# Projection units contraction-outermost, modulation weights in buffers of their own, unread matmuls at the start

## The chip, the cores and the metric

The kernel runs on one core of a Trainium2 chip. The metric is the device time of one execution in microseconds (us). The engines are TensorE (PE; its weight loads are PEld), VectorE (DVE), ScalarE (ACT), GpSimd (POOL) and SyncE (SP), which here only issues DMAs. PSUM has 8 banks of 128 x 512 floats.

## The reference, cut to what matters

One layer of a decoder on 256 prompt tokens and 32 sample tokens (8 sequences of 4), 288 token columns in all, width 1024, everything in float32:

```
mod = silu(c) @ w_ada + b_ada             # 9 rows of c (1 prompt, 8 samples); 6 x 1024 columns
sh1, sc1, g1, sh2, sc2, g2 = mod
h = x * (1 + sc1) + sh1
qa, ka, va, qb, kb, vb, ga, gb = split(h @ w_in)      # 1024 x 5120
... rotary on q and k; dilated window attention (3 groups) and block attention ...
merged = sigmoid(ga) * (oa @ w_pa) + sigmoid(gb) * (ob @ w_pb)
x = LayerNorm(alpha * x + g1 * (merged @ w_o))
f = silu(gt) * up,  up, gt = split((x * (1 + sc2) + sh2) @ w_up)
y = LayerNorm(alpha * x + g2 * (f @ w_down))
```

The first 3072 columns of w_in are q, k and v of the attention: 24 blocks of 128 columns. Blocks 0 to 5 are q of branch A, 6 to 11 k, 12 to 17 v, 18 and 19 q of branch B, 20 and 21 k, 22 and 23 v. The keys, values and window buffers are outputs too.

## The kernel before, in words

Activations lie transposed: width on the partitions (KT = 8 row blocks k), the 288 tokens as columns. A product is made of half units. A half unit gives 128 output columns: for each of the 8 row blocks three matmuls (`mm3`: high part by high part, high by low, low by high), 24 matmuls of 128x128 by 288 into one PSUM bank (`unit_mm`). The weights' high part is a copy that rounds (`w_hi`, ScalarE, `split_hi`), the low part the rest (`w_lo`, VectorE, `split_lo`). Both have 4 places (`SPLIT`) and are made 4 half units ahead (`AHEAD`). The rounded h is `act_hi`, its rest `act_lo`.

Weights come in tiles of 1 MiB: 1024 rows by 256 columns, which are two half units. They go through a ring `raw` of 3 places (`RAW`), in one order of tiles n. SP issues all of them in that order; before each it waits until the place is free (`free_slot`): the tile three before has been split, or, for a tile of adaLN weights, multiplied. The adaLN weights are 24 tiles of the same ring. Tiles 0 to 7 are the adaLN chunks of sh1 and sc1. After them, a w_in tile and an adaLN tile take turns until the 12 w_in tiles of q, k and v are through, with masks, tables and the keys of sequences 0 to 3 in between. The last four adaLN tiles are taken later (`ADA1`, `ADA2`).

An adaLN chunk is multiplied by `ada_mm`: silu(c) as the stationary operand, 32 columns wide, in four column groups of the array, each holding two row blocks. ScalarE copies the bank (`ada_rows`), TensorE adds the four groups and turns the result (`ada_turn`), VectorE adds the bias (`ada_add`) into `mod`.

TensorE's order is written out by hand. At first it turns c, the rows of b_ada and ln1, multiplies chunks 0 to 7 (in the order `ADA_FIRST`), with x turned after the fourth (`turn_x`). VectorE then modulates: h[k] from x, sc1 and sh1, two row blocks a time (`modulate_pair`); ScalarE rounds h (`h_leading`), VectorE makes the rest (`rest_of`). The first half unit needs all 8 row blocks of h, and so all 8 chunks. Then come 12 pairs of half units c, hh into banks 0 and 1, an adaLN chunk and its turn in each pair. A bank is evicted by ScalarE (with rotary work of VectorE and GpSimd behind it for the blocks of q and k), or by VectorE for v. After the last pair TensorE transposes v and k, then the keys of the sample caches, and the attention follows. Later stages wait on counts of these semaphores.

The lines of the profile: L664 to L666 are the three matmuls of `mm3`; L689 `ada_mm`; L697 `ada_turn`; L710 and L713 the turns of c and rows; L718 and L723 `turn_x`; L768 the transposes of v and k; L473 and L478 the splits; L533 the issue of a tile; L1121 `ada_rows`; L1375 `ada_add`; L1387 the modulation; L1392 `rest_of`.

Of the kernel before, what the change touches and what calls it, by code (L numbers as in the profile page):

```python
# [36 lines left out]
SPLIT = 4  # L37
N_ADA0 = 8
MIX0 = N_ADA0
GATE0 = MIX0 + 24  # L40
# [119 lines left out]
ADA_FIRST = (0, 4, 1, 5, 2, 6, 3, 7)  # L160


def ada_chunk(n):

    if n < MIX0:
        return ADA_FIRST[n]
    if n < GATE0:
        return N_ADA0 + (n - MIX0) // 2 if (n - MIX0) % 2 else None
# [17 lines left out]
MIX_N = 12  # L186
# [91 lines left out]
def build(nc, x_prompt, x_sample, cache_a, cache_rows, cache_b, page_table, c_prompt, c_sample, w_ada, b_ada, w_in,  # L278
# [24 lines left out]
    kvin, _ = sb("kvin", [128, 2, 6, 256])  # L303
# [7 lines left out]
    rowbuf, _ = sb("rowbuf", [128, 3, 256])  # L311
# [3 lines left out]
    rows, _ = sb("rows", [64, 128])  # L315
# [42 lines left out]
    st6, _ = sb("st6", [128, 3, 4, 6])  # L358
# [19 lines left out]
    c_zero, c_ready, ada_used, first_in = sem("c_zero"), sem("c_ready"), sem("ada_used"), sem("first_in")  # L378
# [81 lines left out]
    def part(t, slot, by_rows):  # L460
        if by_rows:
            return t[:, slot, :]
        return t[:, slot, :].rearrange("p (k n) -> p k n", k=8)

    def split_hi(act, nb, slot4, rslot, hh, need, by_rows=False):

        if isinstance(nb, int) and nb == 0:
            act.wait_ge(first_in, 16)
        else:
            act.wait_ge(raw_in[rslot], need)  # L470
# [10 lines left out]
    def halves(first, last):  # L481

        out = []
        for n in range(first, last):
            by_rows = PAB0 <= n < WO0 or n >= DOWN0
# [17 lines left out]

    PAB_BANK = (0, 1, 6, 3)
# [14 lines left out]
    def _(sp):  # L519
# [14 lines left out]

        def load_ada(n):
            a = ada_chunk(n)
            load(n, n % RAW, w_ada_v[:, :, 256 * a:256 * a + 256], raw8(n % RAW))

        for n in range(MIX0):
            load_ada(n)  # L540
            if n == 0:
                sp.dma_start(rows[0:48, :], b_ada.rearrange("a (j p) -> (a j) p", p=128)).then_inc(rows_in, 16)
                sp.dma_start(rows[48:56, :], ln1_g.rearrange("a (j p) -> (a j) p", p=128)).then_inc(rows_in, 16)
                sp.dma_start(rows[56:64, :], ln1_b.rearrange("a (j p) -> (a j) p", p=128)).then_inc(rows_in, 16)
            if n == 2:
                sp.dma_start(x_tok[:, 0:2, :], x_prompt.rearrange("a (t p) d -> p (a t) d", p=128)).then_inc(x_in, 16)
                sp.dma_start(x_tok[0:SAMPLE, 2, :], x_sample.rearrange("b t d -> (b t) d")).then_inc(x_in, 16)
# [39 lines left out]
        for n in range(MIX0, GATE0):  # L587
            c = (n - MIX0) // 2
            if n == MIX0:
                free_slot(n)  # L590
                sp.dma_start(raw8(n % RAW)[:, :, 0:128], w_in_v[:, :, 0:128]).then_inc(first_in, 16)
                sp.dma_start(raw8(n % RAW)[:, :, 128:256], w_in_v[:, :, 128:256]).then_inc(raw_in[n % RAW], 16)
                sp.dma_start(cst[:, C_COS:C_MS], const[:, C_COS:C_MS]).then_inc(tables_in, 16)
                sp.dma_start(pages[:], page_table.rearrange("b n -> (b n)").unsqueeze(0)).then_inc(pages_in, 16)
            elif ada_chunk(n) is None:
                load(n, n % RAW, w_in_v[:, :, 256 * c:256 * c + 256], raw8(n % RAW))
            else:
                load_ada(n)
            if n == MIX0 + 9:
                sp.dma_start(cst[:, C_MS:C_END], const[:, C_MS:C_END]).then_inc(masks_in, 16)  # L600
                sp.wait_ge(pages_in, 16)
            if MIX0 + 9 <= n < MIX0 + 9 + DEC_B:
                look_up_pages(n - MIX0 - 9)
            if n > MIX0 + 9 and n % 2 and (n - MIX0 - 11) // 2 < 4:
                load_kv((n - MIX0 - 11) // 2, 0)
# [72 lines left out]
    def ada_bank(i):  # L678
        return {20: 5, 21: 4, 22: 7, 23: 2}.get(i, 5 + i % 3)

    def ada_mm(pe, n):

        i, slot, bank = N_ADA_BEFORE[n], n % RAW, ada_bank(N_ADA_BEFORE[n])
        pe.wait_ge(raw_in[slot], raw_need(n, slot))
        if i >= 3:
            pe.wait_ge(ada_mod, i - 2)
        for k in range(KT):
            q = 32 * (k % 4)
            mm = nc.tensor.matmul(psum[q:q + 32, bank, 0:256], c_z[:, k, :], raw8(slot)[:, k, :], start=(k < 4), stop=(k >= 4),  # L689
                                  skip_group_check=True)  # L690
# [15 lines left out]
    def _(pe):  # L706
        pe.wait_ge(const_in, 16)
# [3 lines left out]
        mm.then_inc(turned_c, 1)  # L711
        pe.wait_ge(rows_in, 48)
# [16 lines left out]
        for i in range(N_ADA0):  # L729
            ada_mm(pe, i)  # L730
            if i >= 1:
                ada_turn(pe, i - 1)
            if i == 3:
                pe.wait_ge(rows_ready, 1)
                turn_x()
        ada_turn(pe, N_ADA0 - 1)

        for c in range(MIX_N):
            for hh in range(2):
                u = 2 * c + hh  # L740
                if c >= 1 and hh == 0 or u == 1:
                    ada_mm(pe, MIX0 + 2 * c + 1)
                if c >= 1:
                    pe.wait_ge(acc_free[hh], c)
                unit_mm(pe, u, u % SPLIT, hh, h_lo if u == 0 else None)
            if c < MIX_N - 1:
                ada_turn(pe, N_ADA0 + c)

        for j in range(8):
            g, hp = j // 2, j % 2  # L750
            if j == 2:
                ada_turn(pe, N_ADA0 + MIX_N - 1)
# [17 lines left out]
        pe.wait_ge(ada_mod, N_ADA0 + MIX_N)  # L770
# [172 lines left out]
        ada_mm(pe, ADA1)  # L943
        pe.wait_ge(o_ready, N_UNITS)
        outputs_turn(1)
        ada_mm(pe, ADA1 + 1)
        ada_turn(pe, 20)


        for h in range(4):  # L950
# [18 lines left out]
            if h == 0:  # L969
                ada_turn(pe, 21)  # L970
# [55 lines left out]
        ada_mm(pe, ADA2)  # L1026
        ada_mm(pe, ADA2 + 1)
        ada_turn(pe, 22)
        ada_turn(pe, 23)


        def first_up_pair():
# [3 lines left out]
            for k in range(KT):  # L1036
                pe.wait_ge(h2_lo, H2_LO_AT[k])
                for q in range(3):
                    wh, wl = part(w_hi, q, False), part(w_lo, q, False)
# [3 lines left out]
            unit_mm(pe, H_UP + 3, 3, UP_BANK[3])  # L1043

        def up_pair(j, second=False):
            for q in range(4):
# [7 lines left out]
                unit_mm(pe, nb, q, q % 2)  # L1054
# [35 lines left out]
        for hcol in range(2):  # L1090
            for kk in range(0, FT if hcol == 0 else FT - 6, 2):
# [5 lines left out]
                if hcol == 1 and kk == 0:  # L1097
                    pe.wait_ge(ada_mod, 24)
# [15 lines left out]
    def _(act):  # L1114
# [12 lines left out]
        for i in range(N_ADA0):  # L1127
            ada_rows(i)
            if i == 4:
                for j in range(2):  # L1130
                    act.wait_ge(turned_x, j + 1)
                    nc.scalar.activation(xT[:, 4 * j:4 * j + 4, 0:128], psum[:, 1 + j, :].rearrange("p (k c) -> p k c", c=128),
                                         ACT.Copy).then_inc(x_ready_act, 1)
            if i == 6:
                for k in range(6):
                    h_leading(k)
        hi_static(act, H_MIX)
        h_leading(6)
        h_leading(7)
        for nb in range(H_MIX + 1, H_MIX + AHEAD):  # L1140
            hi_static(act, nb)

        for c in range(MIX_N):
            for hh in range(2):
                nb = H_MIX + 2 * c + hh
                if c >= 1 and hh == 0:
                    ada_rows(N_ADA0 + c)
# [5 lines left out]
                if nb == H_MIX:  # L1153
                    ada_rows(N_ADA0)
# [54 lines left out]
        for s in range(1, 16):  # L1209
# [77 lines left out]
        ada_rows(22)  # L1287
        ada_rows(23)
# [632 lines left out]
```

## Time and profile before

| | |
|---|---|
| time, median of 3 runs | 564.42 us (560.51 to 568.14) |
| the profiled execution's own time | 561.89 us |
| its span | 560.3 us |
| TensorE matmuls busy | 516.1 us, 92% |
| VectorE, ScalarE, GpSimd busy | 290.5, 223.5, 92.2 us |
| DMA | 116.78 MB, mean 208 GB/s |

The span is what the profiler shows of one execution; all stages below lie on its clock. Busy time of TensorE is the time in which some matmul is under way. Matmuls overlap, so what one costs in a stream is read from the distance of two starts, not from the duration that a row shows. The granted clock is the share of full speed that the record gives for a stretch.

### The profile page before, as it was taken

To read this page: it belongs to the slowest core of one execution; us is meant where nothing else is said; L and a number is where in the kernel's file an instruction comes from. 1 tells how busy PE (TensorE), PEld (TensorE's weight loads), DVE (VectorE), ACT (ScalarE), POOL (GpSimd) and SP (SyncE) were. 2 spreads that over 40 slices of the span, in tenths; PEclk is the share of its full clock that TensorE was granted. 3 is DMA by queue.
4 is the path that set the end of the run, shared out by engine and by line. 5 is a ranking of instruction groups with operands and counts; after the bars stand their busy time and mean duration, and the time that the engine had idled before them with its cause. 6 is when DMAs were issued, how large, how long until landed. Compare 5 with 4: busy or idle time off the path is not lost.

```text
span 560.3 us, 10315 instructions
## 1 busy us (share of the span) xinstructions
PE 516.1 (92%) x4051; PEld 473.0 (84%) x4051; DVE 290.5 (52%) x561; ACT 223.5 (40%) x377; POOL 92.2 (16%) x127
## 2 busy tenths in 40 slices
PE   4787999999999989999989979999999999999990
PEld 2546899989978979897789869999999999999980
DVE  0055657556743453353587595546555544435356
ACT  1042424333344454253643645465444344333311
POOL 1000123002770000000055053601111100000005
PEclk9999899999999999998999979999999999999995
DMA  8987699998185982194433474898876745354002
GB/s 280 340 267 231 208 359 348 338 303 293 38 285 173 303 279 77 42 274 142 151 116 114 148 225 132 302 329 289 264 278 216 272 159 182 120 187 171 17 1 84
DMA packets 96719, 116.78 MB, mean 208 GB/s; under 512 B 3596, under 2 KB 87756, under 8 KB 96165
## 3 DMA queue, kind: packets, MB, share of 16 engines
q1 hardware_dynamic: 94788, 102.76, 56.3%
q0 software_dynamic: 1888, 13.44, 6.6%
q8 instruction: 30, 0.49, 0.4%
q14 instruction: 13, 0.10, 0.1%
HBM read 112.90 MB, written 13.57 MB: 226 GB/s over the span
## 4 chain that ended last, share of the span: by engine, by line
PE 77%; DMA 9%; DVE 4%; ACT 3%; SPq 2%; issue 2%; POOL 2%; POOLq 0%; DVEq 0%; ACTq 0%
PE psum L664 21%; PE psum L666 20%; PE psum L665 20%; DMA raw<-in_w_in 6%; PE psum L689 3%; PE psum L784 3%; DMA raw<-in_w_ada 2%; PE psum L900 2%; PE psum L697 2%; PE psum L844 1%; PE psum L886 1%; DVE w_lo L478 1%; PE psum L853 1%; PE psum L798 1%; ACT qkvg L1206 1%
## 5 line engine op out<-in xcount | busy, mean ns | idle before, releaser
L478 DVE TENSOR_TENSOR w_lo<-raw,w_hi 128x1024 fp32r<-128x1024 f32 x118 | 146.7, 1244 | 169.6 <-ACT w_hi L473 169.4
L664 PE MATMUL psum<-act_hi,w_hi 128*128 128x288 f32 x736 | 223.9, 304 | 9.2 <-DVE act_lo L1647 3.5
L665 PE MATMUL psum<-act_lo,w_hi 128*128 128x288 f32 x736 | 219.6, 298 | 0.0
L666 PE MATMUL psum<-act_hi,w_lo 128*128 128x288 f32 x736 | 219.0, 298 | 0.0
L473 ACT ACTIVATE w_hi<-raw 128x1024 fp32r<-128x1024 f32 x118 | 124.1, 1056 | 138.3 <-PE psum L666 90.7
L664 PEld LDWEIGHTS psum<-act_hi,w_hi 128*128 128x128 f32 x736 | 140.5, 191 | 17.9 <-issue 11.0
L666 PEld LDWEIGHTS psum<-act_hi,w_lo 128*128 128x128 f32 x736 | 141.0, 192 | 0.0
L665 PEld LDWEIGHTS psum<-act_lo,w_hi 128*128 128x128 f32 x736 | 140.8, 191 | 0.1
L664 PE MATMUL psum<-f_hi,w_hi 128*128 128x288 f32 x176 | 52.4, 298 | 0.6 <-DVE f_t L1685 0.6
L665 PE MATMUL psum<-f_lo,w_hi 128*128 128x288 f32 x176 | 51.9, 295 | 0.0
L666 PE MATMUL psum<-f_hi,w_lo 128*128 128x288 f32 x176 | 51.8, 294 | 0.0
L1789 POOL TENSOR_TENSOR qkvg<-qkvg,cst 128x288 f32 (+1 forms) x16 | 16.6, 1036 | 121.0 <-ACT qkvg L1150 121.0
L689 PE MATMUL psum<-raw,c_z 128*32 128x256 f32 x384 | 32.4, 468 | 4.4 <-DMA raw<-in_w_ada 4.3
L664 PEld LDWEIGHTS psum<-f_hi,w_hi 128*128 128x128 f32 x176 | 33.0, 187 | 0.9 <-issue 0.8
L666 PEld LDWEIGHTS psum<-f_hi,w_lo 128*128 128x128 f32 x176 | 33.1, 188 | 0.0
L665 PEld LDWEIGHTS psum<-f_lo,w_hi 128*128 128x128 f32 x176 | 33.0, 188 | 0.0
L1823 POOL TENSOR_TENSOR qkvg<-qkvg,gated 128x288 f32<-128x288 f32 x8 | 8.4, 1079 | 120.0 <-DVE gated L1597 120.0
L697 PEld LDWEIGHTS psum<-cst,rowbuf 128*128 128x128 f32 x96 | 16.0, 235 | 11.9 <-ACT rowbuf L1121 6.2
L1874 POOL DMA_DIRECT2D out<-in_cache_kv_a x24 | 11.7, 488 | 77.4 <-PE psum L666 75.8
L689 PEld LDWEIGHTS psum<-raw,c_z 128*32 128x32 f32 x384 | 11.5, 125 | 13.3 <-DMA raw<-in_w_ada 5.4
L1314 ACT ACTIVATE silu_t<-psum 128x288 f32<-128x288 f32 x22 | 9.0, 409 | 33.5 <-PE psum L666 33.5
L697 PE MATMUL psum<-cst,rowbuf 128*128 128x9 f32 x96 | 16.7, 284 | 5.0 <-ACT rowbuf L1121 5.0
(190 smaller groups left out, 556.4 us busy)
## 6 DMA issues: line engine op xcount, KB each, us to landing
raw<-in_w_ada SPq DMA_DIRECT2D x24, 1024.0 KB, 7.1
raw<-in_w_up SPq DMA_DIRECT2D x22, 1024.0 KB, 7.0
raw<-in_w_in SPq DMA_DIRECT2D x19, 1024.0 KB, 7.0
raw<-in_w_down SPq DMA_DIRECT2D x10, 1024.0 KB, 5.0
out<-in_cache_kv_a POOLq DMA_DIRECT2D x16, 504.0 KB, 6.1
raw<-in_w_o SPq DMA_DIRECT2D x4, 1024.0 KB, 4.8
kvin<-in_cache_kv_a SPq DMA_DIRECT2D x8, 256.0 KB, 3.1
kvin<-in_cache_kv_b SPq DMA_DIRECT2D x16, 128.0 KB, 3.4
```

Of the source, the lines that this page charges most:

```text
L473: nc.scalar.activation(part(w_hi, slot4, by_rows), raw_half(rslot, hh, by_rows), ACT.Copy).then_inc(hi_ready, 1)
L478: nc.vector.tensor_tensor(part(w_lo, slot4, by_rows), raw_half(rslot, hh, by_rows), part(w_hi, slot4, by_rows).bitcast(F32), ALU.subtract) ...
L664: nc.tensor.matmul(out, hi_l, hi_r, start=start, stop=False, skip_group_check=True)
L665: nc.tensor.matmul(out, hi_l, lo_r, start=False, stop=False, skip_group_check=True)
L666: return nc.tensor.matmul(out, lo_l, hi_r, start=False, stop=stop, skip_group_check=True)
L689: mm = nc.tensor.matmul(psum[q:q + 32, bank, 0:256], c_z[:, k, :], raw8(slot)[:, k, :], start=(k < 4), stop=(k >= 4), skip_group_check=True)
L697: mm = nc.tensor.matmul(psum[:, ada_bank(i), 256 + 9 * hh:256 + 9 * hh + 9], rowbuf[:, i % 3, 128 * hh:128 * hh + 128], cst[:, C_ADA:C_ADA ...
L784: mm = nc.tensor.transpose(psum[:, bank, col:col + nr], kv_tiles(b, 0, tile)[0:nr, 0, 128 * hp:128 * hp + 128], cst[0:nr, 0:nr])
L900: mm = nc.tensor.matmul(psum[:, 6, E * i:E * i + E], prbT[:, u % 2, 128 * n:128 * n + 128], tok[:, kb, 1, 256 * g + E * h:256 * g + E * h ...
L1314: nc.scalar.activation(silu_t[:, q, :], psum[:, q, 0:TOK], ACT.Silu).then_inc(silu_ready, 1)
L1789: nc.gpsimd.tensor_tensor(block_at(qkvg, blk), block_at(qkvg, blk), cst[:, C_COS:C_COS + TOK], ALU.mult).then_inc(cos_done, 1)
L1874: pool.dma_start(kv_sample[g][bass.ds(b, 1), 0:BUF[g] - DEC_T, :], cache_rows[g][bass.ds(b, 1), DEC_T:BUF[g], :]).then_inc(moved, 16)
```

## The change

- **Order of the projections.** Blocks 12 to 17 (v of branch A) are made first and together (`first_mm`): for each row block k, the 18 matmuls of six output blocks into six banks (0 to 5). Their weights come in four tiles of two row blocks by 768 columns (`load_first`), split one row block a time. Row block k needs only h[k]. After that come the other nine pairs (`MIX_C`), as before into banks 0 and 1.
- **adaLN weights.** They come as 24 parts of 512 rows by 512 columns, of which the first 20 have five buffers of their own (`ada_s`, laid over memory that is free then, by `ADA_BUF`), and no longer pass through the ring. SP waits for the buffer's last use. Two parts make a chunk of 512 columns: 12 chunks, evictions and `ada_add`s for 24, each with twice as many columns. Chunks 0 and 2 (shift and scale of row blocks 0 to 3) are first.
- **Unread matmuls.** `keep_warm` multiplies the identity with 256 columns into bank 5; nobody reads it. 12 of them stand between the first pieces of work.
- **Order of loads.** The loads of SP up to the first gate tile are written out by hand. The keys of sequences 0 to 3 are loaded after the last adaLN part.
- The four last adaLN tiles stay in the ring, as parts; semaphore counts and places follow.

```diff
+MIX_C = (0, 1, 2, 3, 4, 5, 9, 10, 11)
+FIRST_BLK, FIRST_N = 12, 6
+FIRST_COLS = 128 * FIRST_N
-ADA_FIRST = (0, 4, 1, 5, 2, 6, 3, 7)
+ADA_ORDER = (0, 2, 1, 3, 4, 5, 6, 7, 8, 9, 10, 11)
+ADA_BANK = (6, 7, 6, 7, 6, 7, 6, 7, 6, 7, 5, 7)
+ADA_BUF = (0, 1, 2, 3, 4, 0, 1, 2, 3, 4, 2, 3, 4, 2, 3, 4, 2, 4, 2, 4)
+MIX_ADA = [range(N_ADA0 + (4 * m + 2) // 3, N_ADA0 + (4 * m + 6) // 3) for m in range(9)]
...
+    ada_s = [sb(f"ada_s{i}", [128, 4, 512], F32, o)[0]
+             for i, o in enumerate((o_qkvg + 8 * TOK * 4, o_qkvg + 8 * TOK * 4 + 8192, o_qkvg + 24 * TOK * 4, o_kvin, o_tmp + 4096))]
...
+        def load_start(q):
+            last = [p for p in range(q) if ADA_BUF[p] == ADA_BUF[q]]
+            if last:
+                sp.wait_ge(ada_used, last[-1] + 1)
+            sp.dma_start(ada_s[ADA_BUF[q]][:], ada_part(q)).then_inc(start_in[ADA_BUF[q]], 16)
+
+        def load_first(n):
+            dst = raw[:, n % RAW, 0:2 * FIRST_COLS].rearrange("p (k n) -> p k n", k=2)
+            load(n, n % RAW, w_in_v[:, 2 * n:2 * n + 2, 128 * FIRST_BLK:128 * FIRST_BLK + FIRST_COLS], dst)
+
+        load_start(0)
...
+        load_start(1)
+        sp.dma_start(x_tok[:, 0:2, :], x_prompt.rearrange("a (t p) d -> p (a t) d", p=128)).then_inc(x_in, 16)
+        sp.dma_start(x_tok[0:SAMPLE, 2, :], x_sample.rearrange("b t d -> (b t) d")).then_inc(x_in, 16)
+        load_start(2)
+        load_start(3)
+        load_start(4)
+        load_start(5)
+        load_first(0)
+        load_first(1)
+        load_start(6)
+        load_start(7)
+        load_first(2)
+        load_first(3)
...
+        load_start(8)
+        load_start(9)
+        load_mix(0)
+        load_start(10)
+        load_mix(1)
+        load_mix(2)
+        load_mix(3)
+        load_start(11)
...
+        load_mix(7)
+        load_start(17)
+        load_start(18)
+        load_mix(8)
+        load_start(19)
+        load_kv(0, 0)
+        load_kv(1, 0)
+        sp.wait_ge(ada_used, 19)
+        load_kv(2, 0)
+        sp.wait_ge(ada_used, 20)
+        load_kv(3, 0)
...
+    def ada_mm(pe, q, src, arrived, need):
+        i, a = q // 2, q % 2
+        pe.wait_ge(arrived, need)
+        if a == 0 and i >= 2:
+            pe.wait_ge(ada_mod, i - 1)
+        for kk in range(4):
+            mm = nc.tensor.matmul(psum[32 * kk:32 * kk + 32, ADA_BANK[i], :], c_z[:, 4 * a + kk, :], src[:, kk, :],
+                                  start=(a == 0), stop=(a == 1), skip_group_check=True)
+        mm.then_inc(ada_used, 1)
...
+    def first_mm(pe, k):
+        pe.wait_ge(lo_ready, k + 1)
+        pe.wait_ge(h_lo, k + 1)
+        for q in range(FIRST_N):
+            c = 128 * q
+            mm = mm3(psum[:, q, 0:TOK], w_hi[:, k % SPLIT, c:c + 128], w_lo[:, k % SPLIT, c:c + 128], act_hi[:, k, :], act_lo[:, k, :],
+                     k == 0, k == KT - 1)
...
+        def keep_warm(n):
+            for _ in range(n):
+                nc.tensor.matmul(psum[:, 5, 0:256], ident, cst[:, 0:256], start=True, stop=True, skip_group_check=True)
...
+        keep_warm(4)
...
+        ada_start(pe, 0)
+        keep_warm(2)
+        ada_start(pe, 1)
+        keep_warm(1)
+        ada_turn(pe, 0)
+        keep_warm(2)
+        pe.wait_ge(rows_ready, 1)
+        turn_x()
+        ada_start(pe, 2)
+        keep_warm(2)
+        ada_start(pe, 3)
+        keep_warm(1)
+        ada_turn(pe, 1)
+        ada_start(pe, 4)
+        ada_start(pe, 5)
+        first_mm(pe, 0)
+        ada_turn(pe, 2)
+        first_mm(pe, 1)
+        ada_start(pe, 6)
+        ada_start(pe, 7)
+        first_mm(pe, 2)
+        ada_turn(pe, 3)
+        for k in range(3, KT):
+            first_mm(pe, k)
+
+        for m in range(9):
+            for q in MIX_ADA[m]:
+                ada_start(pe, q)
+            for hh in range(2):
+                nb = H_MIX + 2 * m + hh
+                pe.wait_ge(acc_free[hh], m + 1)
+                unit_mm(pe, nb, nb % SPLIT, hh)
+                if hh == 0 and m in ROWS_AT:
+                    ada_turn(pe, ROWS_AT[m])
```

In ScalarE's and VectorE's order, `hi_static(k)` and `lo_static(k)` of the eight row blocks stand between `h_leading` and `rest_of` of the same row blocks; `modulate_pair(0)` and `(1)` wait for two chunks of `mod`, `(2)` and `(3)` for four. The splits of the first three half units of the pairs stand ahead of the evictions of the six banks, which ScalarE and VectorE share.

## Rows read from the trace of the kernel before

**Rows 1.** The page, busy time of TensorE, us (share) xinstructions.

```profile
PE 516.1 (92%) x4051; PEld 473.0 (84%) x4051; DVE 290.5 (52%) x561; ACT 223.5 (40%) x377; POOL 92.2 (16%) x127
```

**Rows 2.** Windows: stretch, its length, busy us, granted clock, DMA share, GB/s.

```profile
0.00:25.00 25.00, 13.63 (x94) 8.11 (x95) 1.27 (x7) 3.06 (x6) 2.71 (x7) 1.00 0.96 308
25.00:44.00 19.00, 15.06 (x101) 9.31 (x99) 10.26 (x32) 7.12 (x16) 0.00 (x0) 1.00 0.93 286
44.00:54.00 10.00, 9.97 (x64) 9.12 (x64) 5.43 (x8) 2.69 (x4) 0.79 (x1) 1.00 0.57 179
54.00:66.00 12.00, 8.71 (x63) 7.97 (x62) 5.49 (x11) 4.33 (x7) 1.90 (x2) 0.86 0.87 282
66.00:147.00 81.00, 80.30 (x688) 74.01 (x687) 49.39 (x106) 26.98 (x42) 17.44 (x36) 1.00 0.87 289
80.00:115.00 35.00, 35.00 (x301) 32.56 (x299) 20.95 (x43) 11.09 (x18) 7.05 (x6) 1.00 1.05 347
512.00:514.00 2.00, 2.00 (x17) 2.00 (x16) 1.93 (x5) 0.41 (x1) 0.00 (x0) 1.00 0.97 375
```

**Rows 3.** TensorE in order of time, 0 to 45: start, us, instruction, idle before.

```profile
3.85 0.99 PE L710 MATMUL psum<-cst,ctok 9*128 9x9 f32 x8 [3.85 <-DMA ctok<-in_c_sample]
...
23.12 3.65 PE L718 MATMUL psum<-cst,x_tok 128*128 128x128 f32 x16
...
36.15 1.94 PE L689 MATMUL psum<-raw,c_z 128*32 128x256 f32 x16
...
44.03 0.61 PE L664 MATMUL psum<-act_hi,w_hi 128*128 128x288 f32 x1 [3.17 <-DVE w_lo L478]
44.44 0.44 PE L665 MATMUL psum<-act_lo,w_hi 128*128 128x288 f32 x1
44.68 0.44 PE L666 MATMUL psum<-act_hi,w_lo 128*128 128x288 f32 x1
```

**Rows 4.** The same of 57 to 148.

```profile
57.43 0.61 PE L697 MATMUL psum<-cst,rowbuf 128*128 128x9 f32 x4 [3.29 <-ACT rowbuf L1121]
...
58.97 0.40 PE L664 MATMUL psum<-act_hi,w_hi 128*128 128x288 f32 x1
...
66.99 0.51 PE L697 MATMUL psum<-cst,rowbuf 128*128 128x9 f32 x4
67.43 1.07 PE L689 MATMUL psum<-raw,c_z 128*32 128x256 f32 x16
68.43 0.40 PE L664 MATMUL psum<-act_hi,w_hi 128*128 128x288 f32 x1
...
71.72 0.30 PE L664 MATMUL psum<-act_hi,w_hi 128*128 128x288 f32 x1
...
147.09 0.30 PE L666 MATMUL psum<-act_hi,w_lo 128*128 128x288 f32 x1
```

**Rows 5.** Waits of 0 to 160 (total, times, longest); the chain of waits near 108.

```profile
ACT w_hi L473 <- DMA raw<-in_w_in: 39.3, 11, 6.7
...
108.56 8.82 DMA raw<-in_w_in
```

**Rows 6.** VectorE in order of time, 38 to 44.

```profile
38.30 0.74 DVE L1387 TENSOR_SCALAR qkvg<-xT,mod 128x256 f32<-128x256 f32 x2
...
42.76 1.22 DVE L478 TENSOR_TENSOR w_lo<-raw,w_hi 128x1024 fp32r<-128x1024 f32 x1
43.89 0.82 DVE L1392 TENSOR_TENSOR act_lo<-qkvg,act_hi 128x288 fp32r<-128x288 f32 x2
```

**Rows 7.** TensorE in order of time, first pair of the up projection.

```profile
328.02 0.58 PE L664 MATMUL psum<-act_hi,w_hi 128*128 128x288 f32 x1 [3.50 <-DVE act_lo L1647]
...
332.79 0.29 PE L666 MATMUL psum<-act_hi,w_lo 128*128 128x288 f32 x1
332.92 0.29 PE L664 MATMUL psum<-act_hi,w_hi 128*128 128x288 f32 x1
```

**Rows 8.** DMA issues of the page: count, KB each, median us to landing.

```profile
raw<-in_w_in SPq DMA_DIRECT2D x19, 1024.0 KB, 7.0
```

More of the change, by code:

```diff
@@ L465, in split_hi @@
     def split_hi(act, nb, slot4, rslot, hh, need, by_rows=False):
[L467 to L470, printed above, removed]
+        act.wait_ge(raw_in[rslot], need)
         if not isinstance(nb, int) or nb >= SPLIT:
@@ L484, in halves @@
         for n in range(first, last):
-            by_rows = PAB0 <= n < WO0 or n >= DOWN0
+            by_rows = "first" if n < MIX0 else PAB0 <= n < WO0 or n >= DOWN0
             for hh in range(n_halves(n)):
@@ L533, in load, with ada_part @@
             sp.dma_start(dst, src).then_inc(raw_in[slot], 16)
+        def ada_part(q):
+            j, a = ADA_ORDER[q // 2], q % 2
+            return w_ada_v[:, 4 * a:4 * a + 4, 512 * j:512 * j + 512]
         def load_ada(n):
[L536 to L547, printed above, removed]
+            load(n, n % RAW, ada_part(ada_chunk(n)), raw4(n % RAW))
@@ L585, in load_static, with load_mix @@
                 load(n, n % RAW, w_up_v[:, :, col:col + 256], raw8(n % RAW))
[L587 to L605, printed above, removed]
+        def load_mix(m):
+            n, c = MIX0 + m, MIX_C[m]
+            load(n, n % RAW, w_in_v[:, :, 256 * c:256 * c + 256], raw8(n % RAW))
+        load_start(8)
[6 more added lines that the diff above has]
+        load_start(11)
+        sp.dma_start(cst[:, C_MS:C_END], const[:, C_MS:C_END]).then_inc(masks_in, 16)
+        sp.wait_ge(pages_in, 16)
+        look_up_pages(0)
+        look_up_pages(1)
+        load_mix(4)
+        load_start(12)
+        look_up_pages(2)
+        look_up_pages(3)
+        load_mix(5)
+        load_start(13)
+        load_start(14)
+        look_up_pages(4)
+        look_up_pages(5)
+        load_mix(6)
+        load_start(15)
+        load_start(16)
+        look_up_pages(6)
+        look_up_pages(7)
+        load_mix(7)
[9 more added lines that the diff above has]
+        load_kv(3, 0)
         load_static(GATE0)
@@ L1038, in first_up_pair @@
                 for q in range(3):
-                    wh, wl = part(w_hi, q, False), part(w_lo, q, False)
+                    wh, wl = (part(w, (H_UP + q) % SPLIT, False) for w in (w_hi, w_lo))
                     mm = mm3(psum[:, UP_BANK[q], 0:TOK], wh[:, k, :], wl[:, k, :], act_hi[:, k, :], act_lo[:, k, :], k == 0, k == KT - 1)
@@ L1420, in _ @@
+        lo_static(dve, 5)
         rest_of(qkvg, 6, h_hi, h_lo)
         rest_of(qkvg, 7, h_hi, h_lo)
-        for nb in range(H_MIX + 1, H_MIX + AHEAD):
+        for nb in range(6, 11):
             lo_static(dve, nb)
+        for q in (1, 3, 5):
+            if q < 5:
+                dve.wait_ge(first_done, q + 1)
+            else:
+                dve.wait_ge(half_used, KT)
+            V.tensor_copy(qkvg[:, FIRST_BLK + q, :], psum[:, q, 0:TOK]).then_inc(acc_free[1] if q == 1 else v_free, 1)
```

266 lines of the change are left out of this document (135 added, 131 removed).

## The prediction, made before the result was known

> **What bounds the kernel now.** I read the page's busy table first: TensorE works 516 of 560 us [rows 1]. So time can only come from its idle time, from its slow stretches, or from fewer matmuls. The change leaves the real matmuls as they are (118 half units' worth, the same adaLN columns, the same row turns), so I looked for idle and slow stretches with a table of windows by stage [rows 2]. From 66 to 147 us TensorE is busy 80.3 of 81 us. There is nothing to win there but an earlier start. In the first 44 us it is busy 28.7, and with preparations only; from 54 to 66 it is busy 8.7 of 12.
>
> The list of TensorE's instructions in order of time shows what it does [rows 3]. The first projection matmul starts at 44.03, after a wait of 3.17 us for the split weights. Until then it turns and multiplies adaLN chunks as they land, and waits. Neighbouring matmuls of 288 columns are 0.24 us apart there, which is the 1.2 GHz level (288 / 0.24 us), though the granted column says 1.00. Later they are 0.13 us apart, the 2.4 GHz level [rows 7]. The same list from 57 us on gives the prices at the full level [rows 4]: a half unit 3.29 us (68.43 to 71.72), an adaLN chunk 1.00 (67.43 to 68.43), a pair of turns 0.44 (66.99 to 67.43). The stage ends at about 147.2 (last start 147.09). At full price it is 24 x 3.29 + 12 x 1.00 + 11 x 0.44 = 95.8 us; it takes 103.2. The 7.4 lost are the first half unit at the lower level (24 x 0.24 = 5.8 for 3.29), the wait of 3.29 that ends at 57.43 and the slow unit behind it, and a wait near 117. The list of waits has their origin: ScalarE's split waits 39 us in sum for w_in, and one such load took 8.82 us [rows 5].
>
> So the stage ends at (start of projections) + (TensorE's work) + (waits), and the start is set by DMA. 0 to 25 us brings 7.7 MB, and the stream then runs at 347 GB/s where the engines are saturated [rows 2]. All 8 MiB of the adaLN weights of shift and scale, x, and a weight tile must be in first.
>
> **The change, part by part.** All times below are on the clock of the profiled run (span 560.3, time 561.9; the median of the three runs is 564.4, so 2.5 more).
>
> *Start.* The contraction-outermost block k needs only its own h[k] and 768 columns of row block k. h[0..3] need adaLN chunks 0 and 2 (4 MiB), but two more MiB are issued before w_in. The first tile is thus complete after 6.3 MB of adaLN, 1.2 of x, 0.2 of small loads (7.7 MB: 25 us as before) and 0.8 MB more: 25 + 0.79/0.347 = 27.3 us. The new adaLN loads have runs of 2 KB, as w_down's, which reach 375 GB/s in a slice at share 0.97, against 347 at 1.05 for runs of 1 KB [rows 2]. With 375 it is 25.6. I take 26. Split at three quarters of 1.22 us [rows 6] and of the 1.05 that the high part takes, the first projection matmul is at 28.
>
> *Does TensorE get there in time?* The twelve unread matmuls (256 columns, fp32, whole array) have no row. Lower bound: two transposes of 128 columns, 3.65/16 x 2 = 0.46 us at the lower level. Upper: an adaLN part does eight such matmuls in four column groups in 1.94; if the four run at once, one alone is 0.24 x 4 = 0.97 [rows 3]. I take 0.9 at the lower level, 0.45 at the full one, since these are fp32 matmuls and not transposes. Chain at the lower level: c turned at 4.8, four unread 3.6, rows 0.4, chunk part 0 1.9, two unread 1.8, part 1 1.9: 14.4. From there at the full level: unread 6 x 0.45, turns 2 x 0.88, x 2.4, parts 2 x 1.0 = 8.9: 23.3, and modulation 0.2 + 1.2 = 24.7. That is before 28, so the unread matmuls cost nothing; their cover is the arrival of w_in tile 0. At the lower level throughout it is 14.4 + 17.8 + 1.4 + 1.3 (split and rest) = 35: the cover is gone.
>
> *The block of six.* 8 x 18 matmuls. Block 0 at 0.24 us: 28 to 32.3. Turns 1.4: 33.7. Block 1 at full 2.4: 36.1. Adding parts 6 and 7 (landed at 26 + 2.9/0.35 = 34.3) 2.0: 38.1. Block 2: 40.5, turns 41.4, block 3: 43.8. Block 4 waits for the third and fourth chunks: add 0.2, two modulations 2.4 (one is 0.74 [rows 6] and two small steps of the samples, about 0.23 each), split 0.9, rest 0.4: 45.3, a new stall of 1.5 us. Blocks 4 to 7: 54.9. Before, this work (six half units) was done at about 75.
>
> *The nine pairs.* 18 x 3.29 + 12 x 1.00 + 6 x 0.88 = 76.5 us. Evicting six banks at once adds no wait of TensorE: bank 0 is done 2 us before the block ends, and two adaLN parts (2.0 us) come first. DMA has to bring 7.3 MB of w_in, 9.4 of adaLN, 1.3 of masks, 2.9 of keys and 2.1 of gates: 23 MB, 66 us at 347 GB/s, under 76.5. SP's queue is in order, and its tightest place is part 17: it may be issued only when part 15 is used (start of pair 5) and is wanted at the start of pair 6, 8.5 us later; a w_in load's median from issue to landing is 7.0 [rows 8]. Part 18 and the last w_in tile stand behind it. I put 1 us for such waits, between 0 and 7.4, what the old stage lost. End: 54.9 + 76.5 + 1 = 132.4, against 147.2. Gain 14.8.
>
> *The rest.* The key loads 0 to 3 move behind the last adaLN part, 2.9 MB or 8.4 us; the first is wanted some 6 us after the stage's end (the 24 transposes of v and k). The fourth may be issued only when part 19 is used, at the start of the ninth pair (124), some 13 us before it is wanted. I cost this at nothing; the last pair and the transposes cover it, and without them it would be up to those 8.4 us. Later stages move as a block, since their waits count TensorE's progress. The later adaLN turns (20 to 23) become two and save at most 0.9; I take 0. The two doubled semaphore counts, the rowbuf's size and st6's new place: nothing, no engine waits on them.
>
> Sum: 561.9 - 14.8 = 547.1 in a run like the profiled one, 549.6 against the median. I say 548.
>
> **A rule against this change.** The first of the blocks walks six PSUM banks, three matmuls in each. The up projection's first pair walks three banks in the same way, and after 4.4 us at the lower level its matmuls are 0.13 us apart [rows 7], so the trace has no fall with cycling. The Trainium skill, "TensorE: Matmul & The Clock Gate", section "A second HAM failure mode: psum-queue depth-cycling", says that going through PSUM banks makes TensorE micro-idle between groups and swing between its two clock levels. By that rule the sum would be case C below.
>
> **Rivals.**
> A. *The unread matmuls do not raise the clock.* Before, TensorE is busy without a gap from 23 to 39 and a chunk still takes 1.94 at 36.15, not 1.00 [rows 3, 4]; the turns of rows and x are among the new work too. For the full level: the six parts are denser with the unread ones between. Then block 0 starts at 35, not 28: 554.
> B. *Loads arrive just late, or the gain is given back behind the stage.* Part 17 or the last w_in tile costs two waits like that at 54 to 57, or the keys come late: 7 us back, 554.
> C. *Bank cycling.* 144 x (0.24 - 0.133) = 15.4 us: 562, no change.
> D. *Slower.* ScalarE splits weights and evicts banks in one order. A late w_in load blocks its split, the eviction behind it waits, then TensorE, and after a wait of 3 us it runs at the lower level (the unit from 58.97 [rows 4] took 4.8, not 3.3). Price 3.6 + 1.5 = 5.1 us for each pair it hits. The place is SP's queue, where w_in loads now stand behind loads that wait for TensorE's use of an adaLN buffer. It decides from three pairs on (15.3 of 14.8); with five it is 547.1 + 25.5 = 573. Against it: 66 us of DMA in 76.5, and five buffers more.
>
> Chances: forecast 0.60, A 0.17, B 0.10, C 0.05, D 0.08. **Range**: below, no stall at all, 395 GB/s and the 0.9 of the turns: 543; above, A and B with the median's 2.5 and some noise: 560. C and D are left out. **Signs**: 2% of 564.4 is 11.3 us, about what a measurement here can tell, so faster means under 553.1. Forecast nearly all, a bit of B: faster 0.61. A, B, C and the lesser half of D: 0.34. Slower by over 2% needs D in six pairs or more: 0.05.
>
> **What would show it.** Steps right: first projection matmul near 28 with a short wait for w_lo before it; parts 2 to 5 in 1.0 us each, not 1.9 (else A); the ninth pair's end near 132, TensorE nearly gapless from 55 on; a spacing of 0.13 in blocks 1 to 7 (else C). Wrong: waits of TensorE for adaLN parts 16 to 19 or of ScalarE for w_in in the pairs (B, D); a first projection matmul at 35; or the stage ends at 132 while the stretch from there to the end, 413 us now, has grown.

## The result, and the profile after

The changed kernel takes 568.68 us in the median of 4 runs (566.3 to 569.54), the kernel before 563.97 (560.51 to 568.14): ratio 1.0099, 95% interval 1.0058 to 1.014. It is 1% slower; 548 was forecast. The profiled execution of the changed kernel took 566.3 us, span 564.7. All ratios, here and below, leave out an execution that took over 1.5% longer than the fastest of the same kernel; medians and ranges take in every one.

The windows of the changed kernel by stage (stretch, length, busy us of TensorE, its weight loads, VectorE, ScalarE, GpSimd, granted clock, DMA share, GB/s) answer to [rows 2]:

```profile
0.00:25.00 25.00, 18.94 (x113) 11.16 (x113) 3.94 (x13) 3.80 (x6) 2.70 (x7) 1.00 0.92 333
25.00:44.00 19.00, 15.58 (x109) 13.11 (x110) 8.02 (x20) 6.93 (x13) 0.00 (x0) 0.91 1.04 407
44.00:66.00 22.00, 20.43 (x157) 17.85 (x155) 14.31 (x24) 10.88 (x18) 0.80 (x1) 1.00 0.97 336
66.00:124.00 58.00, 58.00 (x440) 50.09 (x440) 39.47 (x84) 19.57 (x30) 12.38 (x14) 1.00 0.76 265
124.00:157.00 33.00, 19.52 (x116) 17.51 (x108) 15.43 (x31) 7.04 (x20) 11.36 (x26) 0.74 0.33 100
```

From 66 to 124 us TensorE works without a gap; then it is busy 19.5 of 33 us, at a clock granted at 0.74. Its instructions in order of time show both parts (they answer to [rows 3, 4]):

```profile
29.48 0.58 PE L721 MATMUL psum<-act_hi,w_hi 128*128 128x288 f32 x1 [3.23 <-DVE act_lo L1493]
...
34.63 0.29 PE L723 MATMUL psum<-act_hi,w_lo 128*128 128x288 f32 x1
34.76 0.29 PE L721 MATMUL psum<-act_hi,w_hi 128*128 128x288 f32 x1
...
136.39 1.88 PE L756 MATMUL psum<-cst,rowbuf 128*128 128x9 f32 x8 [8.39 <-ACT rowbuf L1213]
...
139.71 0.44 PE L721 MATMUL psum<-act_hi,w_hi 128*128 128x288 f32 x1
139.95 0.44 PE L722 MATMUL psum<-act_lo,w_hi 128*128 128x288 f32 x1
...
150.21 0.66 PE L862 MATMUL psum<-cst,qkvg 128*128 128x128 f32 x2 [5.09 <-DVE tok L1592]
...
156.54 1.96 PE L878 MATMUL psum<-cst,kvin 128*128 128x128 f32 x12
```

The first projection matmul starts at 29.48 instead of 44.03. The first half of the ninth pair, the last but one unit, ends near 127.9. One turn (0.9) and one half unit (3.3) are left, so the stage could end at 132.0. Instead TensorE waits 8.39 us for a copy of ScalarE, does most of the last half unit with starts 0.24 us apart (the 1.2 GHz level), ends at 143.2, and after fifteen transposes waits 5.09 us more for VectorE's tok copies, which take the transposed k out of PSUM. The key turns (the transposes of the sample caches' keys) begin at 156.5, where the kernel before began them at 153.0:

```profile
153.00 1.96 PE L784 MATMUL psum<-cst,kvin 128*128 128x128 f32 x12
```

What ScalarE did (L484 is the split, L1255 the eviction, L1213 `ada_rows`):

```profile
120.46 0.41 ACT L1255 ACTIVATE qkvg<-psum 128x288 f32<-128x288 f32 x1 [1.22 <-PE psum L723]
133.55 1.06 ACT L484 ACTIVATE w_hi<-raw 128x1024 fp32r<-128x1024 f32 x1 [12.68 <-DMA raw<-in_w_in]
134.51 0.39 ACT L1255 ACTIVATE qkvg<-psum 128x288 f32<-128x288 f32 x1
134.81 1.05 ACT L484 ACTIVATE w_hi<-raw 128x1024 fp32r<-128x1024 f32 x1
135.75 0.59 ACT L1213 ACTIVATE rowbuf<-psum 128x512 f32<-128x512 f32 x1
```

It waits 12.68 us for a w_in tile, to split it; the eviction of the eighth pair's second bank and the adaLN copy stand behind it in its order. The last half unit needs that bank too, and by the code it is free only when VectorE has read it behind the eviction (L1544, the rotary work), which stands behind the low part of the same split (L489):

```profile
134.64 1.23 DVE L489 TENSOR_TENSOR w_lo<-raw,w_hi 128x1024 fp32r<-128x1024 f32 x1 [10.11 <-ACT w_hi L484]
...
135.79 0.48 DVE L1544 STREAM_SHUFFLE rope_t<-psum 128x288 f32<-128x288 f32 x1
```

SP's queue shows which tile it is, and why it is late:

```profile
119.29 0.97 SPq L600 DMA_DIRECT2D k_early<-in_cache_kv_b  x2
124.68 0.34 SPq L594 DMA_DIRECT2D k_late<-in_cache_kv_a  x1
...
126.27 1.91 SPq L600 DMA_DIRECT2D k_late<-in_cache_kv_b  x2
128.22 1.06 SPq L545 DMA_DIRECT2D raw<-in_w_in  x2
```

It is the first gate tile. Between 120 and 124.7 SP waits for adaLN part 19 to be used, because the keys of sequence 3 go into memory that overlaps that part's buffer; the gate tile stands behind them and leaves at 128.22. The kernel before issued it at 132.93, but 14 us before its stage ended; here it is 4 us before the time at which the stage could have ended. The line of the kernel before:

```profile
132.93 2.09 SPq L533 DMA_DIRECT2D raw<-in_w_in  x2
```

VectorE and GpSimd near the second wait (L1559 are the copies of the last queries, L1921 the scaling of x):

```profile
143.86 5.56 DVE L1559 COPY qz<-qkvg 64x32 f32<-64x32 f32 x4
149.46 0.42 DVE L1591 COPY tok<-psum 128x256 f32<-128x256 f32 x1
```

```profile
142.78 6.04 POOL L1921 TENSOR_SCALAR xT<-xT 128x2304 f32<-128x2304 f32 x1
```

Four copies of 64x32 take 5.56 us. They end when GpSimd's 6 us instruction ends. The tok copies that TensorE waits for come after them. In the kernel before the same four took 0.81 us and were done before the scaling began:

```profile
143.29 0.81 DVE L1443 COPY qz<-qkvg 64x32 f32<-64x32 f32 x4
```

```profile
147.39 6.04 POOL L1809 TENSOR_SCALAR xT<-xT 128x2304 f32<-128x2304 f32 x1
```

### The profile page after: what moved, and what is told of

It reads as the page before. It is cut to its first block, busy times and chain, and to the rows that moved or that the text cites. A ratio compares the mean times of both kernels' runs of the same rounds, so it can differ in the third digit from the quotient of the medians.

```text
span 564.7 us, 9951 instructions
## 1 busy us (share of the span) xinstructions
PE 514.8 (91%) x3883; PEld 468.6 (83%) x3883; DVE 294.7 (52%) x548; ACT 223.1 (40%) x370; POOL 89.3 (16%) x127
## 4 chain that ended last, share of the span: by engine, by line
PE 79%; DMA 8%; DVE 5%; issue 2%; ACT 2%; SPq 2%; POOL 1%; POOLq 0%; ACTq 0%; DVEq 0%
PE psum L721 21%; PE psum L722 20%; PE psum L723 20%; DMA raw<-in_w_in 4%; DMA raw<-in_w_up 3%; PE psum L742 3%; PE psum L878 3%; PE psum L994 2%; PE psum L756 1%; PE psum L980 1%; ACT w_hi L484 1%; PE psum L938 1%; PE psum L947 1%; DVE qz L1559 1%; PE psum L892 1%
## 5 line engine op out<-in xcount | busy, mean ns | idle before, releaser
L489 DVE TENSOR_TENSOR w_lo<-raw,w_hi 128x1024 fp32r<-128x1024 f32 (+1 forms) x120 | 147.1, 1228 | 163.3 <-ACT w_hi L484 163.0
L484 ACT ACTIVATE w_hi<-raw 128x1024 fp32r<-128x1024 f32 (+1 forms) x120 | 124.6, 1041 | 129.1 <-PE psum L723 97.4
L1901 POOL TENSOR_TENSOR qkvg<-qkvg,cst 128x288 f32 (+1 forms) x16 | 14.7, 920 | 118.3 <-ACT qkvg L1255 118.3
L756 PEld LDWEIGHTS psum<-cst,rowbuf 128*128 128x128 f32 x96 | 12.6, 203 | 11.2 <-ACT rowbuf L1213 11.2
L742 PE MATMUL psum<-ada_s,c_z 128*32 128x512 f32 x160 | 20.5, 602 | 1.5 <-DMA ada_s<-in_w_ada 1.4
L756 PE MATMUL psum<-cst,rowbuf 128*128 128x9 f32 x96 | 12.7, 260 | 9.3 <-ACT rowbuf L1213 9.1
L1255 ACT ACTIVATE qkvg<-psum 128x288 f32<-128x288 f32 x16 | 6.5, 408 | 35.2 <-PE psum L723 35.2
```

Of the source, the lines that this page charges most:

```text
L489: nc.vector.tensor_tensor(part(w_lo, slot4, by_rows), raw_half(rslot, hh, by_rows), part(w_hi, slot4, by_rows).bitcast(F32), ALU.subtract) ...
L742: mm = nc.tensor.matmul(psum[32 * kk:32 * kk + 32, ADA_BANK[i], :], c_z[:, 4 * a + kk, :], src[:, kk, :], start=(a == 0), stop=(a == 1), s ...
L756: mm = nc.tensor.matmul(psum[:, ADA_BANK[i], 9 * hh:9 * hh + 9], rowbuf[:, i % 2, 128 * hh:128 * hh + 128], cst[:, C_ADA:C_ADA + 9], start ...
L1901: nc.gpsimd.tensor_tensor(block_at(qkvg, blk), block_at(qkvg, blk), cst[:, C_COS:C_COS + TOK], ALU.mult).then_inc(cos_done, 1)
```

## The experiments

Two causes were to be shown: **G**, the gate tile behind the keys' wait, and **Q**, the copies of the last queries under GpSimd's scaling. Each was taken out of the changed kernel alone (e1; e2 and e6), both together (e3), and each put into the kernel before alone (e8, e7). Ratios are to the kernel before, run on the same chip beside it.

**e1: the gate tile earlier.**

```diff
         load_start(19)
+        load_static(GATE0)
         load_kv(0, 0)
         load_kv(1, 0)
+        load_static(GATE0 + 1)
...
         load_kv(3, 0)
-        load_static(GATE0)
-        load_static(GATE0 + 1)
```

> The changed kernel with one edit in SP's order: the first gate tile is loaded right after adaLN part 19, the second after the keys of sequence 1, so that neither stands behind the wait for part 20. Theory G+Q (two new waits at the end of the pairs; G: the gate tile stands behind the keys' wait, its split blocks ScalarE's evictions; Q: VectorE's copies of the last queries are blocked by GpSimd's scaling of x): ScalarE's wait of 12.7 us for w_in goes, TensorE's wait of 8.4 us too, the ninth pair ends near 132 (now 143.1), but Q stays and still costs TensorE about 5 us and a slow stretch: 10 us less than the changed kernel, 556 to 559. Rival K (the gain cannot be had: the keys come later by as much, or DMA is short there): the key turns wait instead, 564 to 568.

Measured: 553.71 us (546.94 to 559.76), ratio 0.9872 (0.9805 to 0.9939). ScalarE and TensorE:

```profile
122.12 1.06 ACT L484 ACTIVATE w_hi<-raw 128x1024 fp32r<-128x1024 f32 x1 [1.46 <-DMA raw<-in_w_in]
```

```profile
131.71 0.38 PE L862 MATMUL psum<-cst,qkvg 128*128 128x128 f32 x2
...
139.71 0.66 PE L862 MATMUL psum<-cst,qkvg 128*128 128x128 f32 x2 [6.06 <-DVE tok L1592]
```

The wait of 8.4 us is gone, the stage ends at 131.7. The copies of the queries now take 6.54 us, and TensorE waits 6.1 for the tok copies. G is real, and Q stays, as expected. The time is a little below the range and scatters.

**e2: the copies of the last queries after the eighth pair.** The edit is `if m == 8:` to `if m == 7:` before `queries_by_row(3)`.

> The changed kernel with one edit in VectorE's order: the copies of the last queries stand after the eighth pair, not after the ninth. Theory G+Q: TensorE's wait of 5.1 us for the tok copies goes, and the transposes run at 0.11 us a matmul, not 0.21, so 6 to 8 us less than the changed kernel: 560 to 562; the wait of 8.4 us stays. Rival K: GpSimd's scaling blocks another copy of VectorE instead, under 2 us less.

Measured: 559.22 us (558.49 to 561.85), ratio 0.9984 (0.9953 to 1.0015), just below the 560 to 562 expected. VectorE and GpSimd in e2:

```profile
137.88 0.81 DVE L1559 COPY qz<-qkvg 64x32 f32<-64x32 f32 x4
...
143.27 0.43 DVE L1591 COPY tok<-psum 128x256 f32<-128x256 f32 x1
143.61 0.27 DVE L1592 COPY tok<-psum 32x128 f32<-32x128 f32 x1
```

```profile
142.00 6.04 POOL L1921 TENSOR_SCALAR xT<-xT 128x2304 f32<-128x2304 f32 x1
```

The copies take 0.81 us ahead of the scaling. The tok copies, which read PSUM, run at their usual 0.43 and 0.27 us in the middle of it. Of the copies seen here only those from SBUF to SBUF were held up. The wait of 8 us stays; the key turns begin 5.4 us after the stage's end (142.4 to 147.8), not 13.4.

**e3: both.**

> Both edits. Theory G+Q: no wait of TensorE over 1 us between 47 and 150, ninth pair ends near 132, the time is what was predicted for the change, 546 to 552. The two gains add up: 16 to 19 us less than the changed kernel. Rival K: 558 to 568.

Measured: 547.54 us (546.51 to 549.15), ratio 0.9779 (0.9713 to 0.9845). TensorE in e3, at the stage's end:

```profile
124.56 1.06 PE L742 MATMUL psum<-ada_s,c_z 128*32 128x512 f32 x8
128.85 0.96 PE L756 MATMUL psum<-cst,rowbuf 128*128 128x9 f32 x8
132.93 0.38 PE L862 MATMUL psum<-cst,qkvg 128*128 128x128 f32 x2
...
138.32 1.96 PE L878 MATMUL psum<-cst,kvin 128*128 128x128 f32 x12
```

The stage ends at 132.9 without a wait, the key turns begin 5.4 us later. The forecast for the change was 547.1 in such a run, with the stage's end at 132.4: it is the time of this kernel, which differs from the changed one in the places of two loads and of four small copies. That the two agree within 0.5 us is partly luck: the block of six ended 1.9 us later than forecast (56.8, not 54.9), and the nine pairs took 1.4 us less than the 77.5 put down for them and their waits.

**e4: both, without the unread matmuls.** All calls of `keep_warm` are left out.

> Both edits, and the twelve unread matmuls left out. Theory W0 (block 0 waits for DMA and the split anyway; the unread matmuls buy little): the first chunks run at the lower level, block 0 starts 1 to 2 us later than in e3, the time is 0 to 3 us more than e3's. Rival W1 (they carry the start): block 0 starts at 33 or later and the blocks stay slow longer, 5 us or more above e3. Rival W2 (they cost): faster than e3.

Measured: 545.50 us (543.12 to 547.8), ratio 0.974 (0.9667 to 0.9812): by the medians not slower than e3 but 2 us faster, though the two ranges overlap. W1 is out. TensorE in e4:

```profile
7.88 1.93 PE L742 MATMUL psum<-ada_s,c_z 128*32 128x512 f32 x8
11.33 1.94 PE L742 MATMUL psum<-ada_s,c_z 128*32 128x512 f32 x8 [1.51 <-DMA ada_s<-in_w_ada]
13.98 1.88 PE L756 MATMUL psum<-cst,rowbuf 128*128 128x9 f32 x8 [0.72 <-ACT rowbuf L1207]
...
19.91 1.92 PE L742 MATMUL psum<-ada_s,c_z 128*32 128x512 f32 x16
...
25.09 1.07 PE L742 MATMUL psum<-ada_s,c_z 128*32 128x512 f32 x8 [0.48 <-DMA ada_s<-in_w_ada]
```

Parts 0 and 1 run at the lower level (1.93 and 1.94 us), but parts 2 and 3, which take 1.92 us together, and part 5 (1.07) at the full one, with no unread matmul before them; and block 0 starts at 29.38, against 29.48 in the changed kernel. e10 and e11 repeat the pair.

**e5: the block of six waits for all of h.** On e3; in ScalarE's and VectorE's order h[4..7] go ahead of the fifth split.

```diff
-        first_mm(pe, 0)
         ada_turn(pe, 2)
-        first_mm(pe, 1)
         ada_start(pe, 6)
         ada_start(pe, 7)
-        first_mm(pe, 2)
         ada_turn(pe, 3)
-        for k in range(3, KT):
+        pe.wait_ge(h_lo, KT)
+        for k in range(KT):
             first_mm(pe, k)
```

> The kernel with both edits (e3), but the block of six waits for all eight row blocks of h, as the kernel before did: TensorE multiplies and turns chunks 1 and 3 first, ScalarE and VectorE round h[4..7] before the fifth split. Theory O (contraction-outermost order is worth its overlap): the first projection matmul moves from 29.5 to 38 to 40, blocks 1 to 7 run without a stall, the block of six ends at 60 to 62 (now 57), the time is 3 to 6 us above e3's 547.5. Rival N (the order is worth nothing, the early weights and separate buffers are all): within 1.5 us of e3.

Measured: 556.01 us (555.63 to 556.27), ratio 0.9892 (0.9861 to 0.9923), 8.5 us above e3. The first projection matmul moves to 42.6 and the block of six ends at 63.5 (e3: 56.8). Theory O holds, with more than the 3 to 6 us expected. Not all of it is the lost overlap: the third chunk's turn waits 5.64 us for ScalarE's copy, which stands behind the first splits in its order, and the turn behind that wait and part of the adaLN work after it are at the lower level. How much each of these costs was not taken apart.

**e6: the scaling waits for the copies of the queries.** On the changed kernel; one line in GpSimd's order, `pool.wait_ge(qz_ready, 4)`, ahead of the scaling of x.

> The changed kernel with one wait more on GpSimd: it scales x only after VectorE has copied all queries; nothing else is moved. Theory Q (the last queries' copies are blocked by GpSimd's 6 us instruction while it runs): the four copies take 0.8 us, not 5.6, TensorE's wait of 5.1 us for the tok copies goes: 560 to 562. Rival Q2 (the copies stand too late, whatever GpSimd does; the place in VectorE's order is the cause): the copies stay slow or the wait stays, 566 to 569.

Measured: 560.89 us (558.61 to 564.45), ratio 0.9986 (0.9959 to 1.0014). The copies stand where the change put them, and VectorE does them in:

```profile
144.69 0.73 DVE L1559 COPY qz<-qkvg 64x32 f32<-64x32 f32 x4
```

So it is the overlap with GpSimd's instruction and not their place. TensorE's wait for the tok copies falls to 0.3 us, and the key turns begin 5.8 us after the stage's end (144.0 to 149.8).

**e7: the kernel before, with the copies of the queries late.** The edit is `if c == 10:` to `if c == 11:` before `queries_by_row(3)`.

> The kernel before with one edit: the copies of the last queries stand after the twelfth pair, not after the eleventh. Theory Q: they meet GpSimd's scaling (147.4 to 153.4 in the kernel before), one of them takes 4 to 6 us, TensorE waits 4 to 6 us for the tok copies and runs at the lower level behind it: 5 to 9 us above the kernel before. Rival Q2: they take 0.8 us there too, within 1 us of the kernel before.

Measured: 571.16 us (564.91 to 575.5), ratio 1.0125 (1.006 to 1.019). VectorE and GpSimd:

```profile
149.82 6.00 DVE L1443 COPY qz<-qkvg 64x32 f32<-64x32 f32 x4
```

```profile
149.18 6.04 POOL L1809 TENSOR_SCALAR xT<-xT 128x2304 f32<-128x2304 f32 x1
```

The move of these four copies alone makes the kernel before 1.25% slower (9.2 us by the medians, where 5 to 9 were expected). In the profiled execution, at 575.5 us the longest of the four, TensorE waits 5.1 us for the tok copies.

**e8: the kernel before, with the gate tile late.** One line ahead of `load_static(GATE0)`: `sp.wait_ge(ada_used, 20)`.

> The kernel before with one wait more on SP: the first gate tile is issued only when the last adaLN chunk of the pairs is multiplied (about 140.8, before 132.9), as the changed kernel has it by way of the keys' wait. Theory G: ScalarE waits for w_in until about 146 with the eviction of the eleventh pair's second bank behind it, TensorE waits about 3 to 5 us in the twelfth pair: 3 to 7 us above the kernel before. Rival G2 (the slack of the split hides it; the changed kernel's stall has another cause): within 1.5 us.

Measured: 571.85 us (570.13 to 572.18), ratio 1.0167 (1.0131 to 1.0203): 9.9 us more, above the range. ScalarE:

```profile
145.33 1.06 ACT L473 ACTIVATE w_hi<-raw 128x1024 fp32r<-128x1024 f32 x1 [9.68 <-DMA raw<-in_w_in]
146.30 0.39 ACT L1151 ACTIVATE qkvg<-psum 128x288 f32<-128x288 f32 x1
```

TensorE waits 5.0 us for the bank and does the last half unit at 0.247 us a matmul instead of 0.135, 2.5 us more. In the profiled runs the stage's end moves from 147.2 to 154.0, or 6.8 us; the other 3.1 of the 9.9 lie behind it. Over the 100 us from the key turns on the clock was granted at 0.99 and 0.98, against 1.00 in the kernel before; what brought that about was not tested.

**e9: w_in tiles before adaLN parts 4 to 7.** On e4.

```diff
-        load_start(4)
-        load_start(5)
         load_first(0)
         load_first(1)
+        load_start(4)
+        load_start(5)
...
         first_mm(pe, 0)
+        first_mm(pe, 1)
+        ada_start(pe, 4)
+        ada_start(pe, 5)
```

TensorE then does turn 2, parts 6 and 7, turn 3 and the other six blocks.

> The kernel with both edits and without the unread matmuls (e4), with the start reordered: SP loads the first two w_in tiles before adaLN parts 4 to 7, and TensorE makes blocks 0 and 1 before it multiplies those parts. Theory O (after e5, the start is a chain of arrivals that the order of loads sets): block 0 starts at 25 to 26, not 29.4; block 4 no longer waits 1.6 us; the block of six ends 2 to 4 us earlier than in e4, and the time is 1.5 to 4 us less: 541 to 544. Rival L (the eight MiB of adaLN weights set the end of the six, whatever comes first): within 1 us of e4.

Measured: 547.84 us (546.23 to 551.66), ratio 0.9748 (0.9704 to 0.9791). Block 0 starts at 26.6, but blocks 0 and 1 run at 0.21 us a matmul, and the block of six ends at 55.9, as in e4 (55.8), and later than in the second profile of e4's kernel (e10, 53.2). The forecast of 541 to 544 was wrong, and so was rival L: beside e9, e4's kernel was at 545.54 (e10), 2.3 us below it. The forecast had left out that an earlier block 0 is still at the lower level, and that both turns now wait 0.7 us for ScalarE.

**e10 and e11: e4's and e3's kernels again**, five rounds each on one chip.

> e4's kernel once more, beside e3's on the same chip in more rounds. Theory W0: within 1.5 us of e3's kernel. Rival W2 (the unread matmuls cost): 2 us less than it or more. W1 (they save) is out if it is not slower.

> e3's kernel once more, for the comparison with e10 and e9: 546 to 549.

Measured: e10 545.54 us (543.27 to 548.26), ratio 0.9711 (0.9668 to 0.9754); e11 549.53 us (546.49 to 550.53), ratio 0.9762 (0.9722 to 0.9802), a little above the 546 to 549 expected. Over both sets of rounds e4's kernel is at 543.1 to 548.3 in 10 runs, mean 545.7; e3's at 546.5 to 550.5 in 10 runs, mean 548.5. The unread matmuls cost some 2.8 us; W2 holds. In the profiled runs of e10 and e11 block 0 shows it:

```profile
PE psum L721 <- DVE act_lo L1487: 3.2, 2, 1.6
```

```profile
PE psum L721 <- DVE act_lo L1493: 4.8, 2, 3.2
```

These are the waits for the rest of h in e10 and in e11 (total, times, longest). In e10 block 0 starts at 28.3 after 1.6 us of waiting and runs at 0.136 us a matmul, in e11 at 30.0 after 3.2 us and runs at 0.248. In e4's first profile it ran at 0.227, after 3.2 us, and there only 1.1 us is left of the difference at the end of the six. ScalarE had the first tile for its split at 26.0 us in e10, 27.0 in e4 and 27.7 in e11. Why it arrives later or earlier was not settled, and with it why the unread matmuls cost what they do.

## Why the prediction was wrong

**Right, by its own steps.** The first projection matmul was put at 28 and came at 29.5. One us of that is the tile: it was put at 26, from 25.6 at 375 GB/s, but the prediction's own terms give 25 + 0.79/0.375 = 27.1, and ScalarE began to split it at 27.1. The block of six was to end at 54.9 with a new stall of 1.5 us before block 4: it ends at 55.8 with a stall of 1.57. Parts 2 to 5 took 1.0 us each, so the prelude ran at the full level and rival A did not come true. From 25 to 44 us DMA was faster than the 375 GB/s I took: 407. The pairs run without a gap from 55.9 to 127.9, and the stage's end without the stall there is 132.0 in the changed kernel, 131.7 in e1 and 132.9 in e3, against 132.4.

Rival C did not come true. The starts in block 1, with six banks walked, are 0.13 us apart (34.63 and 34.76), and over blocks 4 to 7 they are 0.134 on average. By the Trainium skill, "TensorE: Matmul & The Clock Gate", section "A second HAM failure mode: psum-queue depth-cycling", which reports it of one bf16 kernel with 512 columns, going through banks would have made the clock swing; no run here shows it.

**The step that failed is "The rest": "The key loads 0 to 3 move behind the last adaLN part ... I cost this at nothing".** I asked when the keys are wanted, and they were in time. I did not ask what stands behind them in SP's queue. That is the first gate tile, and its split stands in ScalarE's order ahead of the eviction that has to come before a bank is free, and of the adaLN copy. e1 and e8 show it. Between the changed kernel and e1 the stage's end moves from 143.2 to 131.7. Of these 11.5 us, 8.4 are TensorE's wait and nearly all the rest is the turn and the half unit at the lower level behind it.

It is the mechanism of rival D, at a place of its own. I put D at 0.08, since I looked for it in the pairs' own loads, at 5.1 us a pair with three pairs to break even. One late tile cost twice that, because the wait was not for a delayed arrival but for an event: SP held the tile until TensorE had reached the last pair. "Part 18 and the last w_in tile stand behind it" names the right kind of question, one tile too early. That tile was late too (ScalarE waited 4.5 us at 116.9), and it was hidden.

**The second failure is "Later stages move as a block, since their waits count TensorE's progress".** The copies of the last queries moved from after the last but one pair to after the last, a move of `if c == 10` to `if m == 8` in the diff that I did not cost at all. There they meet GpSimd's scaling of x. The time from the stage's end to the key turns is 5.8 us in the kernel before, 13.4 in the changed one, 14.5 in e1, 5.4 in e2 and 5.4 in e3. So Q costs 8 to 9 us, 5.1 to 6.1 of it the wait and the rest the slow transposes behind it. e6 and e7 show that it is the overlap that does it.

That is what the runs showed of the hardware: a copy of 64x32 from SBUF to SBUF on VectorE, 0.18 us alone, took 4.99 us beside a GpSimd instruction of 6.04 us on SBUF, while VectorE's copies out of PSUM beside it were not slowed. The Trainium skill, "SBUF — State Buffer", section "SBUF: two separate sides", says that VectorE and GpSimd share a pair of ports by an exclusive lock, which a GpSimd instruction, or one of VectorE in a 2-port mode or with two SBUF inputs, holds for its whole length, so that the other one blocks and does not share. By that rule, the trace agrees: the GpSimd instruction ends at 148.82, the copy that it held up at 148.85. In which mode the copies ran no row shows.

**The sum.** On the spans, the changed kernel's 564.7 less e3's 546.0 is 18.7 us. At the key turns the two differ by 18.2 (156.5 and 138.3). 11.5 of G and about 8 of Q make 19.5, less 1.2 by which e3's block of six was later.

| | stage's end | key turns | profiled span | median |
|---|---|---|---|---|
| before | 147.2 | 153.0 | 560.3 | 563.97 |
| changed | 143.2 | 156.5 | 564.7 | 568.68 |
| e1, without G | 131.7 | 146.2 | 558.1 | 553.71 |
| e2, without Q | 142.4 | 147.8 | 558.6 | 559.22 |
| e3, without both | 132.9 | 138.3 | 546.0 | 547.54 |

The medians were measured at several times; the kernel before was at 560.66 beside e1 to e3. e1's profiled execution took 559.76 us, the longest of its five; the other four took 546.94 to 553.79, so its span and its median do not belong together.

**The unread matmuls** were costed at nothing, with the tile's arrival as cover. Block 0 does start at the same time with and without them (29.5 and 29.4), so the cover was there in e4; but over ten runs each they cost 2.8 us, and how is open. Rival A rested on them too, and they were not needed against it in e4, where parts 2 and 3 are at the full level without them; in e10 these two took 3.64 us and only parts 4 and 5 were at the full level. In block 0 the clock was at the lower level in most profiles, with or without them, behind waits of 2.3 to 3.2 us (0.23 to 0.25 us a matmul); in e10, behind a wait of 1.6 us, it was at the full one.

**The best version** is e4's kernel: 545.5 us, 2.6 to 2.9% under the kernel before in two comparisons, and 4% under the changed kernel's 568.68 by the medians.

## What to carry to other kernels

When a load is moved or gets a wait, walk down the issuing queue to the next load whose consumer stands ahead of an eviction in some engine's order; here its lateness, not the moved load's, was the price. A wait for an engine's progress in a queue that should run ahead ties everything behind it to the moment it was meant to prefetch for. A small SBUF-to-SBUF copy on VectorE can be held for the rest of the GpSimd instruction beside it (5 to 6 us in the changed kernel, e1 and e7), so each move of one in the program's order is a step to be costed, however small the copy.

## What the runs showed of the hardware beyond that

After a wait of 8.4 us TensorE ran 24 matmuls at 0.21 us on average, after one of 2.3 to 3.2 us at 0.23 to 0.25, and after one of 1.6 us at 0.13 to 0.14. Loads, mostly of adaLN weights in runs of 2 KB and of w_in in runs of 3 KB, brought 407 GB/s over 19 us at a share of 1.04, against 347 at 1.05 for mostly 1 KB runs in [rows 2].
